# Sliding-window attention of the even layer: the value products of the two units of a query block in one visit

## What is computed

```
z = h @ w_in
u, q, k, v = jnp.split(z, ...)
ya, pool_new = pool_mixer(u, ...)
yb = swa_prompt(q, k, v, sinks)          # 8 query heads, 2 key/value heads, head size 64
y = jnp.concatenate([ya, yb], axis=-1) @ w_out
...
sc = jnp.einsum('bnqhgd,bnkhd->bnhgqk', qc, kb) * scale     # own chunk of 64 and 2 before
p = sink_softmax(sc, sinks)
o = jnp.einsum('bnhgqk,bnkhd->bnqhgd', p, vb)               # the value products
```

## Time and profile before

| | |
|---|---|
| median of 3 runs | 1226.8 us (1226.79 to 1226.83) |
| span of the profiled execution, first to last instruction | 1224.7 us |
| TensorE matmul busy | 1209.1 us, 99% of the span |
| TensorE's share of the chain that ended last | 94% |
| GpSimd, VectorE, ScalarE busy | 65%, 59%, 25% |
| even attention, from the transposes of unit 1 to the end of the last value product | 83.66 to 128.69 us of the span |

### The profile page before, as it was taken

The page is one execution under the profiler, slowest core; times in us unless marked ns, Lnnn a source line. Parts: engine busy times, 40 slices in busy tenths (PEclk is TensorE's granted clock), DMA queues, the critical chain, the costliest instruction groups (busy, mean ns, idle before and its releaser), DMA issues.

```text
span 1224.7 us, 23481 instructions
## 1 busy us (share of the span) xinstructions
PE 1209.1 (99%) x8622; PEld 1143.7 (93%) x8622; DVE 725.1 (59%) x1268; ACT 301.6 (25%) x629; POOL 802.0 (65%) x953
## 2 busy tenths in 40 slices
PE   9999999999999999999999998999999999999997
PEld 8987999999999999999999986899999999999997
DVE  6766677776777622217344579676777777741112
ACT  4035332222222200003111167433222222210001
POOL 7962676767676677777654433477777777667772
PEclk9999999999999999999999999999999999999999
DMA  6221222222222233233231301233222222232321
GB/s 222 95 87 36 74 85 96 87 92 86 86 86 86 89 100 90 99 98 111 88 96 54 106 35 35 71 113 96 87 92 86 86 86 86 87 93 98 103 87 73
DMA packets 35993, 108.99 MB, mean 89 GB/s; under 512 B 6161, under 2 KB 8769, under 8 KB 35937
## 3 DMA queue, kind: packets, MB, share of 16 engines
q1 hardware_dynamic: 29232, 102.14, 25.5%
q10 hardware_dynamic: 6704, 6.04, 1.6%
HBM read 103.04 MB, written 5.13 MB: 88 GB/s over the span
## 4 chain that ended last, share of the span: by engine, by line
PE 94%; DVE 2%; ACT 1%; issue 1%; POOL 1%; DMA 0%; ACTq 0%; SPq 0%; POOLq 0%; DVEq 0%
PE psum L630 18%; PE psum L628 12%; PE psum L629 12%; PE psum L631 12%; PE psum L632 9%; PE psum L600 6%; PE psum L602 6%; PE psum L601 6%; PE psum L1131 1%; PE psum L1133 1%; PE psum L1132 1%; PE psum L927 1%; PE psum L868 1%; PE psum L1100 1%; PE psum L907 1%
## 5 line engine op out<-in xcount | busy, mean ns | idle before, releaser
L500 POOL TENSOR_TENSOR w_lo<-w_raw,w_hi 128x512 fp32r<-128x512 f32 x354 | 487.8, 1398 | 14.8
L630 PE MATMUL psum<-h_both,w_hi 128*128 128x480 f32 x704 | 266.8, 379 | 0.0
L453 POOL TENSOR_TENSOR tick<-tick 1x1 f32<-1x1 f32 x183 | 45.1, 247 | 321.0 <-PE psum L632 204.7
L495 POOL TENSOR_SCALAR w_hi<-w_raw 128x512 fp32r<-128x512 f32 x354 | 219.0, 632 | 0.0
L628 PE MATMUL psum<-h_both,w_hi 128*128 128x304 f32 x704 | 215.8, 307 | 0.0
L629 PE MATMUL psum<-h_both,w_hi 128*128 128x304 f32 x704 | 212.6, 302 | 0.0
L631 PE MATMUL psum<-h_both,w_lo 128*128 128x304 f32 x704 | 210.9, 300 | 0.0
L632 PE MATMUL psum<-h_both,w_lo 128*128 128x240 f32 x704 | 191.5, 272 | 0.0
L632 PEld LDWEIGHTS psum<-h_both,w_lo 128*128 128x128 f32 x704 | 132.0, 188 | 20.5
L600 PE MATMUL psum<-h_both,w_hi 128*128 128x272 f32 x488 | 143.8, 295 | 0.0
L602 PE MATMUL psum<-h_both,w_lo 128*128 128x272 f32 x488 | 141.3, 289 | 0.0
(11 more groups left out here) (312 smaller groups left out, 2455.8 us busy)
## 6 DMA issues: line engine op xcount, KB each, us to landing
w_raw<-in_weights SPq DMA_DIRECT2D x184, 512.0 KB, 3.5
x<-in_x SPq DMA_DIRECT2D x8, 272.0 KB, 6.2
w_raw<-in_weights SPq DMA_DIRECT2D x3, 384.0 KB, 5.9
out_diff_v_new<-odd_dv ACTq DMA_DIRECT2D x1, 1024.0 KB, 5.8
out_diff_k_new<-odd_kT ACTq DMA_DIRECT2D x1, 1024.0 KB, 5.0
out_y<-y_one SPq DMA_DIRECT2D x2, 456.0 KB, 2.5
even_rope<-in_rope ACTq DMA_DIRECT2D x1, 544.0 KB, 4.3
odd_rope<-in_rope ACTq DMA_DIRECT2D x1, 544.0 KB, 3.7
```

Of the source, the lines that this page charges most:

```text
L453: pool.tensor_tensor(tick[:, :], tick[:, :], tick[:, :], ALU.mult).then_inc(ticks, 1)
L495: ins = pool.tensor_scalar(w_hi[:, k, part], w_raw[:, k % RAW, part], 1.0, 0.0, ALU.mult, ALU.add)
L500: ins = pool.tensor_tensor(w_lo[:, k, part], w_raw[:, k % RAW, part], w_hi[:, k, part].bitcast(F32), ALU.subtract)
L630: pe.matmul(two, wh, both[:, :, ONE:T], start=first, stop=False)
```

## The change

In a step u from 1 on, `even_values(u - 1)` stood between the first and the second place for fill tiles; unit 9's stood behind the loop. Now no value product is made in an even step, and an odd step ends with those of both units of its block, `even_values(u - 1)` and `even_values(u)`. Nothing is added or removed on any engine, and the orders of VectorE, ScalarE, GpSimd and SyncE stay as they were.

```
@@ -938,16 +938,17 @@
                 if u:
                     even_turns(u)
                     even_fill(u, 0)
+                even_fill(u, 1)
+                if u + 2 < len(EU):
+                    even_scores(u + 2)
+                even_fill(u, 2)
+                if u % 2:
                     if u == 1:
                         pe.wait_ge(even_x_half, 1)
                     if u == 3:
                         pe.wait_ge(x_upd, 1)
                     even_values(u - 1)
-                even_fill(u, 1)
-                if u + 2 < len(EU):
-                    even_scores(u + 2)
-                even_fill(u, 2)
-            even_values(9)
+                    even_values(u)
```

## The result

| | before | changed |
|---|---|---|
| median | 1226.86 us (1226.46 to 1227.12, 8 runs) | 1230.24 us (1229.32 to 1232.49, 8 runs) |
| span of the profiled execution | 1224.7 us | 1227.2 us |
| ratio | | 1.0029, 95% interval 1.002 to 1.0038 |

The changed kernel is slower by 3.4 us in the median. Its runs are spread wider than those of before: four lie between 1229.3 and 1229.6 with a mean granted clock of TensorE of 0.998 to 0.999, four between 1230.9 and 1232.5 with 0.995 to 0.997. The profiled execution is one of the first group (1229.42 us).

What follows compares the result with a forecast made beforehand. The prediction took TensorE, busy for 99% of the span, to bound the kernel. Its eight step terms summed to +2.77 us, taken as 2.7 on the median of 1226.8: 1229.5 us, range 1227.5 to 1231.0.

Steps and rivals of the forecast that it cites:

- Border of a visit: TensorE's switch into and out of value products: 0.35 us between fills, 0.30 taken where a transpose follows, bounds 0.15 to 0.35.
- double visit: Value products of both units of a block in a row, ahead of transposes: 2.03 us, for block 0 1.17.
- steps 1, 3 and 5: Odd steps, each from one unit's transposes to the next's, that end with joined products: +1.17, +0.81 and +1.55 us.
- Step 1: Transposes of unit 1 to unit 2: unit 3's scores still wait for ScalarE's copy, joined products follow: +1.17 us.
- Steps 2 and 4: Transposes of units 2 to 3 and 4 to 5: ScalarE and VectorE's cycle binds, freed time becomes idle: 0.00 and -0.16 us.
- Step 5: Transposes of unit 5 to unit 6: joined products +0.81, later transpose half +0.17, a wait 0.47, restart 0.10: +1.55 us.
- wait for the add: In step 5 the fifth fill tile waits for VectorE's add of the half four tiles earlier: 0.47 us.
- the restart of 0.10: In step 5, a cold restart of TensorE behind the fifth fill tile's wait: 0.10 us.
- Steps 6, 7, 8: From unit 6's transposes to the projection behind the attention: -1.22, +1.63 and -1.01 us.
- The gain: Rival over the attention: fewer borders and all waits covered, 4 x 0.35 us saved, 1225.4 us; chance 0.06.
- The case in which the waits bind less: Rival: step 5's fifth tile does not wait and the border ahead of a transpose is 0.15: 1228.0 us; chance 0.22.
- the falling clock: Rival: idle time ahead of unit 3's transposes drops TensorE from 2.4 to 1.2 GHz, 3 us more, 1232.5 us; chance 0.10.

Runs made afterwards that it cites:

- refilled: Changed kernel with seven fill tiles moved into the waits of steps 2, 4, 5 and 7, all blocks still joined: 1226.99 us, ratio to before 1.0001.
- late_blocks_merged: Kernel before with products joined only for blocks 2 and 3, and fill tiles moved in or into steps 2, 5 and 7: 1225.91 us, ratio 0.9992.
- changed_again: The changed kernel measured once more without an edit: 1231.16 us median of 6 runs.
- first_block_merged: Kernel before with only block 0's value products joined, at the end of step 1: 1229.72 us median of 11 runs.
- step2_refilled: Changed kernel with three fill tiles moved from step 3 to the end of step 2, all else as in it: 1228.60 us.
- all_but_first: Kernel before with the value products of blocks 1 to 4 joined and block 0's where they stood: 1228.72 us.

## Why the prediction was right, and where it was off

**Bound.** TensorE's delay came through to the end: +2.74 in the attention, +2.5 in the span, +2.6 in the runs of the lower group. The rest of the difference in the span is 0.26 us by which T1 itself came earlier, ahead of the change. That nothing behind gives time back was right. The sum came out within 0.03 because its terms are off by up to 0.07 in both directions and cancel; as an account it is good to about 0.1 a step, not to 0.03.

**Border of a visit.** Forecast 2.03 for a double visit. In the changed profile the last fill matmul ahead of V2 and V3 starts at 99.43, the products at 99.65 and T4 at 101.52: 2.09 less the usual 0.125 is 1.97. The border ahead of a transpose is thus 0.24, in the bounds of 0.15 to 0.35, a little under the 0.30 taken. It is the reason why steps 1, 3 and 5 came out 0.05 to 0.07 below their terms. The far side of a visit ahead of a transpose is indeed cheaper than ahead of a fill.

**Step 1.** S3 starts at 84.68, 1.28 behind T1, as before: bound by the copy, with 0.69 us of idle time where V0 stood. Right.

**Steps 2 and 4.** The cycle from T to T is 5.32 and 5.33 (forecast 5.26 and 5.27), with waits of 1.72 and 0.88 (forecast 1.8 and 1.0). Right.

**Step 5.** The wait for the add is there. It is listed with 0.31 us, counted from the modelled end of the fill matmul at 109.32. Counted from start to start, as the forecast does, the next fill matmul comes at 109.92 instead of 109.45: 0.47, as forecast, and the restart of 0.10 is there too (0.23 to the next start instead of 0.125). The 0.05 that the step lacks is the border.

**Steps 6, 7, 8.** -1.17, +1.62 and -1.02, within 0.05 of the terms; S9 is 123.52 - 119.29 = 4.23 behind T7, where 4.10 was derived.

**The rivals.** The gain needed T3 less than 5.0 us behind T2; it is 5.32. Its mechanism, fewer borders, is real: refilled and late_blocks_merged show it as soon as the waits are covered. The case in which the waits bind less did not occur.

**What was off: the clock.** The prediction has the falling clock as a rival with 0.10. It reads 1.59 us of idle time in 7 us at full clock as evidence against it, and speaks of pauses of this size. That step failed. The 1.59 us are a sum of several gaps; the longest single wait in that stretch, and in the whole profile before, is

```profile
755.44 0.40 PE L1131 MATMUL psum<-y_both,w_hi 128*128 128x272 f32 x1 [1.25 <-DVE y_both L2115]
```

so no row showed what a pause of 1.7 us does. And one stretch in one execution shows that the clock can stay up, not that it does. In the changed order it fell behind the 1.7 us wait in the profile of changed_again, and 9 of the 14 runs of the two measurements lie in the upper group. The forecast, 1229.5, is the lower group (1229.3 to 1229.6); the median of 1230.24 has the clock in it. That it still lies inside the range is luck in part: four of its eight runs were in the upper group. In changed_again it was five of six, and the median of 1231.16 lies above the 1231.0 at which the range ends. The price was over-sized: 1.42 us for the fall that was profiled, not 3, since the clock was back after 3.4 us. Of the causes, the one long wait is what the runs point to: first_block_merged has that wait and no other over 0.7, and eight of its eleven runs lie higher; step2_refilled has all others, and one of eleven does. That the fall costs 1.4 us is shown in one execution; that the other high runs are the same fall at the same place is inferred from their times, which come and go with the wait, and not shown. Within the upper group, the three runs at 0.997 take 1230.93 to 1231.01, as the profiled one. Those at 0.996 and 0.995 take 1231.3 to 1232.5; the early fall between 7 and 12 us beside the one in the attention would explain some tenths of a us more, but none of them was profiled, and what makes two of them 2.5 to 3 us longer than the lower group stays open.

## What to carry to other kernels

Work between two dependent steps on the busiest engine is cover as well as cost. Before joining it elsewhere, go through each place that it leaves and ask what the next instruction waits for, and when that is ready; the time stays only where the wait is shorter than what is left between. If independent work can be cut into pieces of known length, move it into the gaps in the same edit: seven fill tiles decided here between +2.7 and 0 us in the attention. A kernel whose busiest engine works for 98% of the span can still lose its clock in one long pause, so compare the spread of the runs, not only the median. The mean granted clock of a run says that there was a fall somewhere; where it was, only a profile says, by its busy time stretch by stretch from the start on. When rows are taken as evidence on pauses, the longest single one counts, not their sum.

## What the runs showed of the hardware that was not expected

- TensorE's granted clock can fall right behind a wait of 1.7 us between busy stretches (0.90 and 0.68 as means of the two stretches of 4 us around it, 1.00 before and after). It does so in some executions of one program and not in others. The wait of 1.24 to 1.25 us that ends at 755 to 759 us was followed by full clock in all nine profiles. The Trainium skill, "TensorE: Matmul & The Clock Gate", section "HAM oscillation — how this bites in real kernels", warns only of longer pauses; here the measurement decides, and a pause of 1.7 us was enough. In the five versions whose waits in the attention are 0.9 us or less, three of 55 runs stand apart from the rest (1230.23 in all_but_first, 1229.9 in step2_refilled, 1227.85 in late_blocks_merged), and one of 54 of the kernel before beside them.
- The length of a pause alone doesn't decide. In the first 8 us of the program TensorE waits for GpSimd's weights. In five profiles the clock falls behind this wait, which is 0.55 to 1.35 us long there (0.69 as the mean from 6.5 to 12 us); in the other four it is 0.62 to 1.11 us long and the clock stays at 1.00. What else decides is not known.
- Changing between full-width matmuls and the value products, which use 64 columns, has a cost at each border: 0.35 us per visit between fills, 0.24 where a transpose follows.
